# RG-LRU pieces handed to the engines in groups of four or five beside the RWKV recurrence, instead of one at a time

## The chip, the cores and the metric

The kernel runs on one core of one Trainium2 chip. The metric is the device time of one execution in microseconds (us), as the median of several. The names used for the engines are those of the profile: PE is the matmul engine (TensorE) and PEld its weight loads, DVE is VectorE, ACT is ScalarE, POOL is GpSimd, and SP is the engine that issues most transfers. Each engine runs its own instruction list strictly in order and waits for the others through semaphores.

## What is computed

One layer of a hybrid backbone over 128 context tokens and 1024 latent tokens, all in f32. A modulated input is projected; three mixers work on the columns of the projection (RWKV-7, RG-LRU and Mamba-2 SSD, each in both time directions); their outputs are projected, normalised, and sent through a mixture of 16 experts. Only two mixers matter here:

```python
# RWKV-7, per head and per direction, one step in time
sa = einsum('bhvk,bhk->bhv', s, -kk_t)
s = s * w_t + sa[..., None] * (kk_t * a_t) + v_t[..., None] * k_t
y_t = einsum('bhvk,bhk->bhv', s, r_t)
# RG-LRU, 768 channels, per direction
rg = sigmoid(blockdiag(w_a) @ xc + b_a);  ig = sigmoid(blockdiag(w_x) @ xc + b_x)     # xc: width-4 conv of xb
log_a = -8 * rg * softplus(-lam)
u = sqrt(-expm1(2 * log_a)) * (ig * xc)
h = linear_recurrence(exp(log_a), u, h0)          # h_t = a_t h_(t-1) + u_t
y = (h_forward + h_backward) * gelu(gb)
```

## The kernel before

The program runs nine stages one after the other, with a barrier between them: modulation, input projection, RWKV features, RWKV recurrence, RWKV output, SSD, output projection, experts, final norm. The change touches the recurrence stage alone (`rwkv_recurrence`), and in it only the second of its two runs: `rc` treats the 2 chunks of 64 context tokens with nothing beside it; `rs` treats the 16 chunks of latent tokens and computes the whole RG-LRU mixer (`Lru`) beside the recurrence.

**The recurrence.** Per chunk there are 25 named products, in this order: T Tt Bt A2 W2 X2 Y2 W4 X4 Y4 W8 X8 Y8 W16 vT X16 Y16 W32 R Y32 kT U bT Yo S. PE issues each for the two time directions one behind the other (chains g = 0 and 1). A plain product is 16 matmuls of 64x64 per direction; A2, R and S have twice as many and Yo three times. Every product has one taker that copies it out of PSUM: ACT for the X's and Y's, vT, kT, bT and Yo, DVE for all others. X needs the W of its level, the next W needs that X, and the next X and Y need the Y. `rs` gives three PSUM banks to each direction, so a product may not start before the one three places earlier has been taken. Every engine walks through the same 25 names of a chunk in the same order; one name of one chunk is a *slot*, 16 x 25 = 400 slots in all.

**The RG-LRU beside it.** `Lru` is written as one generator per engine, each of which yields 140 times: one opening piece, 23 pieces for each of six column blocks j, and one closing piece. Piece *j.v* of one engine belongs to piece *j.v* of the others, and semaphores join them. What a piece holds:

- v = 0 to 11: PE one gate product (128x128 weights, 384 columns, two PSUM banks in turn, so product w waits for the sigmoid of w-2) and ACT its sigmoid out of PSUM (L563). At v = 0 that sigmoid also waits for the output *y* of the block before. DVE does the four convolution steps of block j+1 at v = 3, 5, 7, 9; POOL multiplies at v = 6 and 12.
- v = 12 to 15, ACT on 128x1152: gelu and th0; th1 and av0; av1 and sq0; sq1.
- v = 15, 16, DVE: q0 (after sq0), q1 (after sq1). v = 16, 17, ACT: root0 (after q0), root1 (after q1).
- v = 17, DVE: u0 (after root0). v = 18: u1 (after root1) and the two scans of the forward direction. v = 19: the two scans of the backward direction. v = 20: two small copies and the sum. v = 21: y.
- SP loads the next inputs at v = 10, 12 and 22 and stores y at v = 22.

The opening piece computes constants (ACT, then DVE) and the whole convolution of block 0 (DVE).

`Aside` decides when pieces are issued. PE, ACT, DVE and POOL each own one and call its `turn()` once at the end of every slot, behind their instructions of that slot. So a piece's instructions stand in the engine's list between the recurrence's instructions of this slot and of the next. SP calls it 25 times in a row for each chunk, ahead of its wait for the end of that chunk and the loads of the chunk after next. Before the change `turn()` issues piece number floor(140 * slot / 400): one piece every two or three slots.

Of the kernel before, what the change touches and what calls it, by code (L numbers as in the profile page):

```python
# [73 lines left out]
class Chain:  # L74
# [5 lines left out]
    def turn(self, i, start=0):  # L80

        self.n, self.base = 0, start + i * self.per
# [334 lines left out]
class Aside:  # L417
# [5 lines left out]
    def turn(self):  # L423

        self.slot += 1
        while self.piece < self.pieces * self.slot // self.slots:
            self.piece += 1
            next(self.program)
# [249 lines left out]
def ssd(nc, d):  # L678
# [8 lines left out]
    with ExitStack() as stack:  # L687
# [156 lines left out]
        with ExitStack() as inner:  # L844
# [26 lines left out]
            def skewed(first, second, third, eng):  # L871

                def turn(c, b):
                    first(c + 1, 1 - b)
                    third(c - 1, 1 - b)
                    second(c, b)
                first(0, 0)
                first(1, 1)
                second(0, 0)
                with eng.Fori(0, NT // 2 - 1) as i:  # L880
                    for b in range(2):
                        turn(2 * i + b + 1, 1 - b)
                turn(NT - 2, 1)
                third(NT - 2, 1)
                second(NT - 1, 0)
                third(NT - 1, 0)
# [1266 lines left out]
def routing(nc, d, keep, raw, raw_in):  # L2153
# [3 lines left out]
    with ExitStack() as stack:  # L2157
# [56 lines left out]
        def _(pe):  # L2214
# [22 lines left out]
            def turn_gates(t):  # L2237
                pe.wait_ge(dve_g.sem, dve_g.at("aff", t))
                if t:
                    pe.wait_ge(dve_a.sem, dve_a.at("affT", t - 1))  # L2240
                pe_a.done(pe.transpose(ap[0:E, 0:P], aff[:, t % 2], ident[:]), "affT")
            turn(0)
            for t in range(NT):
                if t + 1 < NT:
# [624 lines left out]
```

## Time and profile before

| | before |
|---|---|
| median of three runs | 5324.62 us (5320.96 to 5327.24) |
| profiled execution, its time | 5324.72 us |
| its span in the trace | 5323.0 us |
| `rs`, first matmul to the last instruction on DVE's state | 1793 to 2406 us, 613 us |
| share of busy time in the whole span | PE 80%, PEld 63%, DVE 46%, ACT 29%, POOL 10% |

The span is what the trace covers; 1.7 us of the execution lie around it. The busy shares are means over nine stages with different limits. What is changed lies in the 613 us of `rs`, 11.5% of the span.

### The profile page before, as it was taken

What the parts mean: (1) busy time and instruction counts of PE and PEld (TensorE: products, weight loads), DVE (VectorE), ACT (ScalarE), POOL (GpSimd) and SP (SyncE); (2) the same over time, 40 slices, a digit from 0 to 9 for tenths busy, and PEclk for the clock granted to TensorE, in tenths of its full rate; (3) what the DMA queues carried; (4) which work ended last, traced back from release to release, by engine and by line L of the source; (5) the groups of instructions that cost most, each with busy time, mean ns of one, the idle gap of its engine ahead of it and who ended that gap; (6) DMA issues with size and microseconds to landing.
All of it is one profiled execution on the core that took longest, in us unless ns stands there. A gap on an engine that the chain in (4) does not pass through costs nothing. (4 is left out here: it accounts for less than half of the span.)

```text
span 5323.0 us, 87271 instructions
## 1 busy us (share of the span) xinstructions
PE 4268.0 (80%) x38736; PEld 3342.1 (63%) x38736; DVE 2439.8 (46%) x2312; ACT 1553.5 (29%) x1654; POOL 514.2 (10%) x298
## 2 busy tenths in 40 slices
PE   4599999998444789992265699974999999999990
PEld 1599999998112688881154344463777777777760
DVE  2410010010664355454665232327666666666667
ACT  0111111110221254450222100012555555555540
POOL 0200000000132111111010000000010100101003
PEclk7799999999666899996556899976999999999995
DMA  8522222221776222223521631144888888988876
GB/s 317 186 73 62 62 73 63 62 73 41 283 285 230 62 56 73 56 48 110 158 80 36 225 112 67 70 150 159 290 299 295 295 298 294 304 291 297 295 240 244
DMA packets 560198, 893.45 MB, mean 168 GB/s; under 512 B 147123, under 2 KB 323663, under 8 KB 533375
## 3 DMA queue, kind: packets, MB, share of 16 engines
q1 hardware_dynamic: 517708, 794.76, 43.9%
q10 hardware_dynamic: 32964, 56.31, 2.8%
q0 software_dynamic: 9216, 37.75, 2.8%
q8 instruction: 255, 4.18, 0.3%
q14 instruction: 55, 0.44, 0.0%
HBM read 745.15 MB, written 143.58 MB: 167 GB/s over the span
## 5 line engine op out<-in xcount | busy, mean ns | idle before, releaser
L2615 DVE TENSOR_TENSOR ex_lo<-moe_raw,ex_hi 128x2048 fp32r<-128x2048 f32 x384 | 879.7, 2291 | 417.0 <-ACT ex_hi L2551 416.8
L2551 ACT ACTIVATE ex_hi<-moe_raw 128x2048 fp32r<-128x2048 f32 x384 | 735.4, 1915 | 578.3 <-PE ex_bank L2493 351.6
L379 PE MATMUL feat_acc<-proj_hH,feat_wH 128*128 128x384 f32 x2112 | 706.5, 335 | 12.6 <-DVE feat_wL L362 12.6
L379 PE MATMUL feat_acc<-proj_hL,feat_wH 128*128 128x384 f32 x2112 | 706.3, 334 | 0.0
L379 PE MATMUL feat_acc<-proj_hH,feat_wL 128*128 128x384 f32 x2112 | 706.2, 334 | 0.0
L362 DVE TENSOR_TENSOR feat_wL<-proj_raw,feat_wH 128x2048 fp32r<-128x2048 f32 (+1 forms) x44 | 99.0, 2253 | 962.1 <-ACT feat_wH L334 962.1
L2090 PE MATMUL op_acc<-op_w,op_yT 128*128 128x512 f32 x1152 | 496.5, 594 | 25.3 <-DMA op_w<-in_w_out 25.3
L2090 PEld LDWEIGHTS op_acc<-op_w,op_yT 128*128 128x128 f32 x1152 | 219.5, 191 | 301.8 <-issue 301.8
L379 PEld LDWEIGHTS feat_acc<-proj_hH,feat_wH 128*128 128x128 f32 x2112 | 397.1, 188 | 13.0 <-DVE feat_wL L362 13.0
L379 PEld LDWEIGHTS feat_acc<-proj_hL,feat_wH 128*128 128x128 f32 x2112 | 397.1, 188 | 0.0
L379 PEld LDWEIGHTS feat_acc<-proj_hH,feat_wL 128*128 128x128 f32 x2112 | 397.0, 188 | 0.0
L2493 PE MATMUL ex_bank<-ex_hi,ex_xH 128*128 128x512 f32 x1024 | 328.2, 402 | 14.5 <-DVE ex_lo L2615 12.9
L340 ACT ACTIVATE feat_out<-feat_acc 128x1152 f32<-128x1152 f32 (+1 forms) x44 | 49.9, 1135 | 938.6 <-PE feat_acc L379 938.6
L2493 PE MATMUL ex_bank<-ex_lo,ex_xH 128*128 128x512 f32 x1024 | 317.2, 391 | 0.0
L2493 PE MATMUL ex_bank<-ex_hi,ex_xL 128*128 128x512 f32 x1024 | 316.2, 390 | 0.0
L2493 PEld LDWEIGHTS ex_bank<-ex_hi,ex_xH 128*128 128x128 f32 x1024 | 184.2, 188 | 83.9 <-issue 27.6
L2515 PE MATMUL ex_bank<-moe_raw,ex_xce 128*32 128x256 f32 x4096 | 234.3, 381 | 0.0
L2493 PEld LDWEIGHTS ex_bank<-ex_lo,ex_xH 128*128 128x128 f32 x1024 | 192.8, 188 | 41.8
L2493 PEld LDWEIGHTS ex_bank<-ex_hi,ex_xL 128*128 128x128 f32 x1024 | 192.6, 188 | 41.4
L2515 PEld LDWEIGHTS ex_bank<-moe_raw,ex_xce 128*32 128x32 f32 x4096 | 126.6, 110 | 99.5 <-issue 22.5
L1434 PE MATMUL rf_mod_acc<-rf_wq,rf_sil 128*32 128x512 f32 x512 | 88.8, 798 | 124.7 <-DMA rf_wq<-in_w_mod 124.7
L2493 PE MATMUL ex_bank<-ex_hi,ex_hH 128*128 128x512 f32 x512 | 167.5, 408 | 0.0
(417 smaller groups left out, 6083.7 us busy)
## 6 DMA issues: line engine op xcount, KB each, us to landing
moe_raw<-in_w_gate SPq DMA_DIRECT2D x256, 512.0 KB, 8.2
moe_raw<-in_w_up SPq DMA_DIRECT2D x256, 512.0 KB, 9.9
moe_raw<-in_w_down SPq DMA_DIRECT2D x256, 512.0 KB, 7.4
rf_wq<-in_w_mod SPq DMA_DIRECT2D x64, 1024.0 KB, 9.9
proj_raw<-in_w_in SPq DMA_DIRECT2D x43, 1024.0 KB, 5.5
mod_slab<-in_w_mod SPq DMA_DIRECT2D x8, 4096.0 KB, 30.9
scratch_FEAT<-feat_out ACTq DMA_DIRECT2D x43, 576.0 KB, 2.8
rr_feat<-scratch_RW SPq DMA_DIRECT2D x144, 128.0 KB, 3.0
```

What stands on the lines that cost most here:

```text
L340: act.activation(out[0:m, k].rearrange("p (g c) -> p g c", g=NSEG), acc[k][0:m, :, 0:SEG], ACT.Copy).then_inc(copied, 1)
L362: dve.tensor_tensor(wL[:, k, :, 0:m], raw[:, k, :, 0:m], wH[:, k, :, 0:m], ALU.subtract).then_inc(low, 1)
L379: last = pe.matmul(acc[k][:, g, 0:SEG], a[:, k, t, :], b[:, t, cols], start=t == 0 and j == 0, stop=t == KT - 1 and j == 2)
L1434: last = pe.matmul(mod_acc[j % 2][32 * g:32 * g + 32, :], sil[:, k, :], wq[:, u % MRING, g * MW:(g + 1) * MW], start=k == 0, stop=k == KT ...
L2090: last = pe.matmul(acc[slot][:, q, :], yT[:, slot, k, :], w[:, k, q * 512:(q + 1) * 512], start=k == 0, stop=k == KT - 1)
L2493: last = pe.matmul(main(ph)[b][:], m[:, k, :], w[:, slot, a, 512 * b:512 * (b + 1)], start=i == 0 and a == 0 and j == 0, stop=i == top and ...
L2515: last = pe.matmul(ctx(ph)[32 * j:32 * j + 32, 0:256], x, raw[:, n % NRAW, a, 256 * j:256 * (j + 1)], start=i == 0 and a == 0, stop=i == t ...
L2551: act.activation(hi[:, n % NS], raw[:, n % NRAW], ACT.Copy).then_inc(hi_made, 1)
L2615: dve.tensor_tensor(lo[:, n % NS], raw[:, n % NRAW], hi[:, n % NS], ALU.subtract).then_inc(lo_made, 1)
```

## The change

Two lines are added in `Aside.turn`. A slot whose number is not a multiple of twelve now issues nothing, except the last, number 400. At slots 12, 24, ..., 396 and 400 the loop catches up, so that each engine issues four or five pieces (the first group four with the opening piece; the last two) one behind the other.

```diff
@@ class Aside
     def turn(self):
         self.slot += 1
+        if self.slot % 12 and self.slot < self.slots:
+            return
         while self.piece < self.pieces * self.slot // self.slots:
             self.piece += 1
             next(self.program)
```

As 12 does not divide 25, the groups fall behind changing names of the chunk. Which pieces each group holds (slot, product of that slot, pieces; the groups that hold only pieces v = 0 to 11 are left out):

```
 12 X8   opening, 0.0-0.2      192 Y16  2.16-2.19            312 X8   4.12-4.15
 48 bT   0.11-0.14             204 A2   2.20-2.22, 3.0       324 Yo   4.16-4.19
 60 Y4   0.15-0.19             240 vT   3.9-3.13             336 W8   4.20-4.22, 5.0
 72 U    0.20-0.22, 1.0        252 Tt   3.14-3.17            372 U    5.10-5.13
108 W4   1.9-1.12              264 W16  3.18-3.21            384 X4   5.14-5.17
120 Y32  1.13-1.17             276 T    3.22, 4.0-4.2        396 kT   5.18-5.21
132 Y2   1.18-1.21             144 R    1.22, 2.0-2.2        400 S    5.22, closing
180 W2   2.11-2.15
```

No instruction is added or removed, and the order of each engine's pieces among themselves stays.

## Rows read from the trace of the kernel before

**Rows 1.** Busy time by stretch: us, PE, PEld, DVE, ACT, POOL, PE clock, DMA, GB/s.
```profile
1793.00:2406.00 613.00, 553.95 (x15505) 500.80 (x15505) 307.95 (x586) 289.44 (x570) 88.40 (x80) 0.95 0.25 61
...
1900.60:1904.60 4.00, 3.99 (x74) 3.99 (x76) 1.76 (x4) 1.41 (x4) 0.00 (x0) 0.50 0.01 4
```

**Rows 2.** Waits of PE, 1790 to 2410: total us, times, longest us.
```profile
PE rs_bank L1709 <- DVE rr_W L1837: 34.2, 17, 10.8
PE rs_bank L1709 <- DMA rr_rt<-scratch_RT: 9.5, 1, 9.5
PE rs_bank L1709 <- ACT rr_X L1779: 8.9, 4, 4.8
PE rs_bank L1709 <- ACT rr_Y L1779: 8.1, 4, 2.9
PE rs_bank L1709 <- issue: 2.7, 7, 0.5
PE rs_bank L1709 <- DVE rr_Tt L1830: 2.3, 3, 1.4
PE rs_bank L1709 <- DVE rr_U L1839: 1.0, 1, 1.0
```

**Rows 3.** Timeline of PE at the stage's start: start, us, idle before.
```profile
1811.26 1.97 PE L1709 MATMUL rs_bank<-rr_W,rr_Y 64*64 64x64 f32 x32 [10.75 <-DVE rr_W L1837]
```

**Rows 4.** Timeline of DVE around the scans of block 0.
```profile
1893.76 1.35 DVE L635 TENSOR_TENSOR lru_th<-lru_th,lru_ig 128x1152 f32<-128x1152 f32 x1
1895.02 0.42 DVE L643 TENSOR_TENSOR_SCAN lru_rg<-lru_av,lru_th 128x128 f32<-128x128 f32 x1
...
1897.60 0.40 DVE L643 TENSOR_TENSOR_SCAN lru_rg<-lru_av,lru_th 128x128 f32<-128x128 f32 x1
...
1900.16 0.73 DVE L1837 TENSOR_TENSOR rr_W<-rs_bank,rr_masks 128x256 f32<-128x256 f32 x2
```

**Rows 5.** Timeline of PE behind the same scans.
```profile
1900.61 1.97 PE L1709 MATMUL rs_bank<-rr_W,rr_Y 64*64 64x64 f32 x32 [4.17 <-DVE rr_W L1837]
...
1905.73 1.10 PE L1709 MATMUL rs_bank<-rr_ident,rr_feat 64*64 64x64 f32 x32
1906.67 1.10 PE L1709 MATMUL rs_bank<-rr_W,rr_Y 64*64 64x64 f32 x32
...
1908.53 1.10 PE L1709 MATMUL rs_bank<-rr_X,rr_Tt 64*64 64x64 f32 x32
```

**Rows 6.** Timeline of ACT over pieces 0.12 and 0.13.
```profile
1865.16 1.28 ACT L567 ACT_TABLE_LOAD   x1
...
1868.67 0.64 ACT L1779 ACTIVATE rr_X<-rs_bank 128x256 f32<-128x256 f32 x2
...
1869.72 1.27 ACT L572 ACTIVATE lru_th<-lru_rg,lru_sp 128x1152 f32<-128x1152 f32 x1
...
1873.47 0.64 ACT L1779 ACTIVATE rr_Y<-rs_bank 128x256 f32<-128x256 f32 x2
```

**Rows 7.** Instruction groups by shape in the stage: busy us, mean ns, idle before.
```profile
L563 ACT ACTIVATE lru_rg<-lru_bank,lru_bias 128x384 f32<-128x384 f32 x36 | 20.9, 581 | 46.9 <-PE lru_bank L534 46.8
...
L584 ACT ACTIVATE lru_th<-lru_th 128x1152 f32<-128x1152 f32 x12 | 13.9, 1164 | 5.2 <-DVE lru_th L651 5.1
...
L651 DVE SCALAR_TENSOR_TENSOR lru_th<-lru_rg,lru_th 128x1152 f32<-128x1152 f32 x12 | 16.7, 1394 | 1.6 <-ACT lru_rg L577 1.4 <-ACT lru_rg L580 0.2
...
L613 DVE SCALAR_TENSOR_TENSOR lru_cv<-lru_xb,lru_par,lru_cv 128x1155 f32<-128x1155 f32 x12 | 17.8, 1484 | 0.1
```

**Rows 8.** Timeline of PE around one gate product.
```profile
1817.86 1.15 PE L1709 MATMUL rs_bank<-rr_W,rr_Y 64*64 64x64 f32 x32
1818.93 0.91 PE L534 MATMUL lru_bank<-lru_xc,lru_gates 128*128 128x384 f32 x2
1819.78 1.15 PE L1709 MATMUL rs_bank<-rr_Y,rr_W 64*64 64x64 f32 x32
```

**Rows 9.** The page's costliest groups: matmuls of the same width back to back.
```profile
L379 PE MATMUL feat_acc<-proj_hH,feat_wH 128*128 128x384 f32 x2112 | 706.5, 335 | 12.6 <-DVE feat_wL L362 12.6
```

## The prediction

> **What bounds the kernel now.** Only the 613 us of `rs` can change, so I read the windows first: PE is busy for 554 of them, at a mean granted clock of 0.95 [rows 1]. So PE sets the time, and what the change can give or take is PE's idle time, the clock behind it, and the price of single PE instructions. Next come PE's waits: 66.7 us in seven lines [rows 2]. Of these 9.5 are the first load, which stays. The longest wait for DVE, 10.75 us, stands at the first W product, while the opening piece runs [rows 3]. The other 46.4 us are what today's spread pieces cost in idle time. The timeline shows how one of them arises. u1 and the four scans of block 0 occupy DVE from 1893.76 to 1900.16, 6.4 us in one lump; W8 stands behind them in DVE's list, is taken at 1900.16, and PE goes on at 1900.61 after 4.17 us of idling [rows 4, 5]. So a lump on DVE is hidden as far as PE has products that don't need it, here 2.2 us, and the rest is lost. PE is then slow too: the granted clock is 0.50, the 1.2 GHz level [rows 1], and three products take 5.12 us, where the next three take 2.80 [rows 5], so 2.3 us more are lost. A plain product thus costs 0.93 us for both directions, A2, R and S 1.87, Yo 2.8.
>
> A check of this reading: 21 plain products, three double and one triple make 28 us, with some 1 us of short waits 29 per chunk and 464 for 16. A gate product delays PE by 1.92 - 0.93 = 0.99 us [rows 8], 72 of them 71. Idle time behind the first load is 57. A clock of 0.95 means 61 us at the low level; some 17 of those are the opening, and at the rate of 2.3 lost of 5.1 the others cost 20. The sum is 612 of 613 us.
>
> **The change, part by part.** No instruction comes or goes; what changes is how many pieces stand in a row between two slots.
>
> *Groups with pieces 0 to 11 only.* PE has four or five gate products in a row, and ACT four or five sigmoids of 0.58 us [rows 7]. PE isn't idle there, so DVE's one or two convolution steps, at most 1.48 us each [rows 7], are hidden behind about 3.2 us of gate products. Without that cover each pair would cost up to 3 us. Gate products behind each other can save PE something. Nothing saved is one bound. The other is the projection's matmul of the same width, 335 ns in a stream [rows 9]; a gate product is two such instructions, 0.67 us, which saves 0.32. Between them stands the chain of two banks: a gate product of 0.91 [rows 8], its sigmoid of 0.58 and some 0.05 of signalling make 1.54 per two, so 0.77, which saves 0.2. I take that: 72 products in 23 groups leave 49 that follow another, 49 x 0.2 = -10 us (0 to -16).
>
> *The opening.* It moves from slot 3 to slot 12, by when its loads have landed. But ACT's constants now stand behind the taking of X8. From the end of X8: 0.6 for the taking, 2.0 on ACT (a table load of 1.28 [rows 6] and three short steps), 0.9 for five short steps on DVE and 5.3 for the convolution (four steps of at most 1.48 [rows 7], the first and last shorter), then a late first sigmoid, 1.1; the short ones are estimates. That is 10 us against 10.75 [rows 3]: 0 (-3 to +3).
>
> *Heavy groups.* Prices on ACT: v = 12 takes 3.5 us from its table load to the next taking, v = 13 3.75 [rows 6]; v = 14 2.3 and v = 15 1.15 at the same pace; a table load and root0 1.28 + 1.16 [rows 6, 7]. On DVE: q and u 1.35 each [rows 4, 7], two scans 2.58 [rows 4], v = 20 1.5 and v = 21 1.3, by the same width. I count from the end of the slot's product on PE; taking it ends some 0.6 later (an estimate from 0.73 us for both directions [rows 4], the first of which is taken while the second is multiplied). From the start of a taking to the matmul that needs it is 0.45 us [rows 4, 5].
>
> Three groups in full. **Slot 60 (Y4, pieces 0.15 to 0.19)**: ACT 0.6, sq1 1.15, load and root0 2.44, so 4.2; DVE then u0, to 5.5, and the lump of 6.4, to 11.9; only then does it take W8. PE has W8 to multiply, 0.93, and X8 needs it taken: idle 11.9 + 0.45 - 0.93 = 11. **Slot 120 (Y32, 1.13 to 1.17)**: ACT 0.6, th1, load, av0, av1, sq0, to 6.6; q0 on DVE to 7.9; load and root0 to 10.4; u0 to 11.7. Behind these stand the takings of kT and U. PE has kT, U and bT, 2.8, and Yo needs U: 9.5. **Slot 132 (Y2, 1.18 to 1.21)**: DVE has u1, four scans, the sum and y, 9.3 us, in front of W4. It began behind W2; PE has X2, Y2 and W4: 7.
>
> The others in the same way. ACT's lump in front of Yo (slot 48): 5; of X4 (108): 2.5; X2 (180): 10; X16 (240): 6; bT (372): 4.5. Both engines in turn, in front of W32 (192): 8.5; Bt (252): 5, as DVE has no slack there; W16 (312): 9; S (324): 9.5; W8 (384): 6.5. DVE alone in front of W32 (264): 4.5; of U (396): 6.5. The groups in which y meets the next block's first sigmoid (72, 204, 336): 1, 2, 3; a sigmoid table load in front of two waiting gate products (144, 276): 1 each. Together with 11, 9.5 and 7 that is 113 us against 46.4 today: **+67**. If PE covers 1 us more or less in each of the 20, 20 us either way.
>
> *Clock.* Fourteen of these stalls are over 4 us, like that of rows 5, and I charge each 2.3 us: 32, against the 20 of today: **+12** (0, if no stall adds a low stretch, to +20). The Trainium skill, "TensorE: Matmul & The Clock Gate", section "Why this matters for your kernels", advises against idle gaps between bursts of matmuls because the clock falls back; by it every heavy group, not fourteen, would be charged, some 14 us more. The trace agrees for the gap of 4.17 us and shows the clock restored within six.
>
> The table loads are as many as before. The same skill, "ScalarE: Activation LUTs", section "What ACT_TABLE_LOAD costs", puts 2.66 us on a switch, drain included; by it the loads in my lumps would cost some 20 us more. The row shows 1.28 us, with the next work right behind [rows 6], and the sum goes by it.
>
> *SP and POOL.* SP issues its pieces ahead, before the end of the chunk; grouping delays them by at most eleven slots, and the nearest use (gb from v = 22 to v = 12 of the next block) is more than thirty slots off. POOL's multiplications are used four pieces later or more. Both at 0, by that distance; a load that came late would stop PE for its few us once per block.
>
> **Sum.** 67 + 12 - 10 + 0 = +69. The profiled execution took 5324.7 us, span and 1.7 us around it, as the median of the three runs does: 5324.7 + 69 = **5394 us**.
>
> **The rivals.**
> *Half of it is covered.* What ACT does in the lumps might be hidden by PE's look-ahead of three banks, so that only DVE's lumps count. The five ACT groups (28 us) and about 15 of the mixed ones would go: 5394 - 43 = 5351. For it: ACT waits for PE most of the time. Against it: X's wait for ACT reached 4.8 us [rows 2] with single pieces already. Chance 0.08.
> *Faster: one interruption instead of four.* Place: PE at the 23 groups with gate products. Their spacing falls to 0.67, 16 us less, and a group would disturb the level chain once where four pieces do so four times. It decides as soon as the stalls sum to under 62 us, 3 per heavy group instead of 5.6; with today's 46 the time is 5324.7 - 16 = 5309. For it: 34.2 us of waits for DVE in 17 places [rows 2]. Against it: most of today's pieces cost nothing, as one alone fits into the 2.2 us that PE covers, and four don't. Chance 0.07.
> *The clock doesn't come back.* Stalls come every 12 to 25 slots; where two follow each other closely the clock may stay low throughout the products between. Twelve products cost 11 us at full clock, and at the rate of rows 5 some 9 more; for the ten groups that follow a stall, less the 2.3 charged, +67: 5461. Against it: three products were enough. Chance 0.04.
> *Nothing changes*, since the waits in the pieces order the engines whatever their place: 5325. PE's idling at the lumps speaks against it. Chance 0.03.
>
> **How the numbers follow.** My forecast has 0.78. Its own terms reach from 67 - 20 - 16 - 3 + 0 = +28 to 67 + 20 + 3 + 20 = +110, and not all ends meet. The range 5350 to 5440 takes in the half-covered case and leaves out the clock's, the faster one's, no change and the tails, together 2 in 10. A difference of 0.2% (10.6 us) is about what a measurement of this kernel can tell from none. Faster 0.06 (the faster rival, where it exceeds that bound), same 0.04, slower 0.90.
>
> **What the profile after would show.** PE's waits in `rs` at about 133 us in place of 66.7, in some 20 places of 2 to 11 us at the slots named, the longest behind slot 60; the mean clock of the stage near 0.93; gate products 0.8 us apart inside a group; the same busy times on ACT, DVE and POOL; the other stages unmoved. The prediction is wrong if the lumps run while PE is still busy (PE's waits near 66 us), if the gate products gain more than they lose, or if the opening stalls PE for much more than 10 us.

## The result, and the profile after

The changed kernel takes 5407.8 us against 5323.4, 1.0163 times as long (95% interval 1.0145 to 1.0181); measured again beside later experiments, 1.0155 (1.0136 to 1.0175). It is 84 us slower, where 69 were forecast, and inside the range.

`rs` as a whole, by the windows (columns as in [rows 1]):

```profile
1790.00:2485.60 695.60, 560.67 (x15505) 516.24 (x15505) 312.14 (x587) 292.50 (x570) 84.33 (x80) 0.90 0.22 54
```

The stage now takes 695.5 us instead of 613.1, so it holds the whole loss. The busy times of DVE and ACT are nearly what they were (312 and 293 us against 308 and 289); the mean granted clock went from 0.95 [rows 1] to 0.90. PE's waits, which answer to [rows 2]:

```profile
PE rs_bank L1711 <- DVE rr_W L1839: 63.1, 20, 11.3
PE rs_bank L1711 <- ACT rr_X L1781: 20.2, 4, 9.8
PE rs_bank L1711 <- DVE rr_U L1841: 15.4, 2, 9.0
PE rs_bank L1711 <- DMA rr_rt<-scratch_RT: 9.5, 1, 9.5
PE lru_bank L536 <- DVE lru_xc L623: 8.6, 1, 8.6
PE rs_bank L1711 <- DVE rr_S L1846: 8.2, 1, 8.2
PE rs_bank L1711 <- ACT rr_yo L1773: 4.8, 1, 4.8
PE rs_bank L1711 <- issue: 4.6, 5, 2.3
PE rs_bank L1711 <- ACT rr_bT L1781: 4.5, 1, 4.5
PE lru_bank L536 <- ACT lru_rg L565: 2.7, 2, 1.4
```

They sum to 141.6 us instead of 66.7, and they name new places: S, Yo and bT, takings that stand behind a group; U rises from 1.0 to 15.4. The timeline of PE at some of them (idle time before the instruction in brackets):

```profile
1845.58 1.15 PE L1711 MATMUL rs_bank<-rr_W,rr_Y 64*64 64x64 f32 x32 [1.51 <-DVE rr_W L1839]
...
1903.76 1.98 PE L1711 MATMUL rs_bank<-rr_W,rr_Y 64*64 64x64 f32 x32 [11.28 <-DVE rr_W L1839]
...
1936.77 1.15 PE L1711 MATMUL rs_bank<-rr_W,rr_Y 64*64 64x64 f32 x32
1937.85 3.14 PE L536 MATMUL lru_bank<-lru_xc,lru_gates 128*128 128x384 f32 x8
1940.92 1.15 PE L1711 MATMUL rs_bank<-rr_Y,rr_W 64*64 64x64 f32 x32
...
2003.64 0.48 PE L1711 MATMUL rs_bank<-rr_A,rr_U 64*64 64x64 f32 x4 [9.02 <-DVE rr_U L1841]
...
2026.54 1.97 PE L1711 MATMUL rs_bank<-rr_W,rr_Y 64*64 64x64 f32 x32 [6.94 <-DVE rr_W L1839]
...
2190.69 1.23 PE L1711 MATMUL rs_bank<-rr_W,rr_Y 64*64 64x64 f32 x32 [2.74 <-DVE rr_W L1839]
```

The three groups worked out in full, slots 60, 120 and 132, were forecast at 11, 9.5 and 7 us and measure 11.28, 9.02 and 6.94. Four gate products in a row take 1940.92 - 1937.85 = 3.07 us, 0.77 each. Counted as [rows 8] were, from the product ahead to the one behind, they delay PE by 1940.92 - 1936.77 - 0.93 = 3.22 us, where four single ones cost 4 x 0.99 = 3.96. What the stall behind slot 60 is made of shows on ACT and DVE, whose lines alternate:

```profile
1891.87 1.25 ACT L582 ACTIVATE lru_rg<-lru_rg,lru_nsp 128x1152 f32<-128x1152 f32 x1
1893.13 1.28 ACT L586 ACT_TABLE_LOAD   x1
1894.43 2.22 ACT L586 ACTIVATE lru_th<-lru_th 128x1152 f32<-128x1152 f32 x2
```
```profile
1893.15 1.36 DVE L653 SCALAR_TENSOR_TENSOR lru_th<-lru_rg,lru_th 128x1152 f32<-128x1152 f32 x1 [2.01 <-ACT lru_rg L582]
1895.62 2.63 DVE L637 TENSOR_TENSOR lru_th<-lru_th,lru_ig 128x1152 f32<-128x1152 f32 x2 [1.12 <-ACT lru_th L586]
1898.17 0.42 DVE L645 TENSOR_TENSOR_SCAN lru_rg<-lru_av,lru_th 128x128 f32<-128x128 f32 x1
...
1903.30 0.73 DVE L1839 TENSOR_TENSOR rr_W<-rs_bank,rr_masks 128x256 f32<-128x256 f32 x2
```

sq1, the load and the roots on ACT; q1, u0, u1 and the scans on DVE, each waiting for the other; then W8 is taken, at 1903.30.

To compare kernels I split the stage of each profiled execution in three, by windows of 2 us: PE idle; PE busy at the low clock level, counted as busy time x (1 - granted clock); and the rest, which is PE's work at full clock. Time outside the stage differs by up to 30 us between executions, whatever the kernel, so the stage says more than the total where little is at stake.

| us | stage | idle | lost to the clock | rest |
|---|---|---|---|---|
| before | 613.1 | 59.1 | 22.1 | 531.9 |
| after | 695.5 | 134.8 | 42.1 | 518.6 |
| after, again | 690.1 | 135.0 | 34.8 | 520.3 |
| only gate products grouped | 615.9 | 72.2 | 21.2 | 522.5 |
| only long pieces grouped | 678.0 | 119.1 | 31.9 | 527.0 |
| groups every six slots | 638.2 | 84.6 | 30.5 | 523.1 |
| after, PE kept busy | 672.0 | 61.4 | 12.7 | 597.8 |
| after, short scans | 664.3 | 109.1 | 35.0 | 520.3 |
| after, 2.11 earlier | 683.3 | 127.3 | 35.8 | 520.2 |
| gates only, short POOL work | 617.1 | 70.6 | 24.0 | 522.6 |
| placed | 553.2 | 25.0 | 3.0 | 525.1 |
| placed, tables earlier | 549.1 | 18.3 | 2.9 | 527.9 |

Between before and after: idle +75.7, clock +20.0, rest -13.3, together +82.4. The loss of the clock varies with the execution, as the repeat shows; idle time and rest don't.

### The profile page after: what moved, and what is told of

It is laid out like the page before. It is cut to its first block and busy times, and to the rows that moved or that the text cites. A ratio compares the mean times of both kernels' runs of the same rounds, so it can differ in the third digit from the quotient of the medians.

```text
span 5406.2 us, 87271 instructions
## 1 busy us (share of the span) xinstructions
PE 4289.3 (79%) x38736; PEld 3368.9 (62%) x38736; DVE 2444.3 (45%) x2312; ACT 1556.4 (29%) x1654; POOL 510.4 (9%) x298
## 5 line engine op out<-in xcount | busy, mean ns | idle before, releaser
L1436 PE MATMUL rf_mod_acc<-rf_wq,rf_sil 128*32 128x512 f32 x512 | 92.2, 828 | 119.1 <-DMA rf_wq<-in_w_mod 119.1
```

The source lines that it names most:

```text
L1436: last = pe.matmul(mod_acc[j % 2][32 * g:32 * g + 32, :], sil[:, k, :], wq[:, u % MRING, g * MW:(g + 1) * MW], start=k == 0, stop=k == KT ...
```

## The experiments

Where pieces are given other slots, a table replaces the formula (`UPTO`, the number of pieces issued by the end of each slot; `self.slots` is 400 here):

```diff
-        while self.piece < self.pieces * self.slot // self.slots:
+        while self.slots == 400 and self.piece < self.pieces and UPTO[self.slot] > self.piece:
```

**Only the gate products, only the long pieces.** In the first, pieces v = 0 to 11 go to multiples of twelve (at the latest with v = 12), in the second v = 12 to 22. In both the opening piece stays at slot 3.

> Only the pieces v = 0 to 11 are collected at multiples of twelve slots; v = 12 to 22 stay one at a time. Theory (what costs is the lump of long ACT and DVE work in front of an awaited taking; gate products in a row are 0.79 us apart instead of 0.99): 48 of 72 gate products follow another, -10 us, idle time of PE near the 66.7 us of before, so 5314 us (5305 to 5322). Rival (every interruption costs, whatever it holds, so fewer turns are better): about 17 us less idle time as well, 5297. Rival (groups of gate products stall PE at their two banks): slower than before, 5335 or more.

> Only the pieces v = 12 to 22 are collected at multiples of twelve slots; gate products are issued one at a time. Theory (the long lumps carry the whole loss, the gate groups gave 10 us back): the time after plus 10, 5418 us (5405 to 5430), with PE's waits near 140 us. Rival (the gate groups carry the loss): 5325 to 5340.

Gates alone: 1.0008 (0.9997 to 1.0019). Long pieces alone: 1.0127 (1.0108 to 1.0145), some 68 of the 84 us (in the stage 64.9 of 82.4), and the gate groups don't carry the loss. Neither met its number. With gates alone the rest fell by 9.4 us, close to the 10 expected, but idle time rose by 13.1. Its waits:

```profile
PE rs_bank L1729 <- DVE rr_W L1857: 40.3, 20, 9.3
PE rs_bank L1729 <- ACT rr_Y L1799: 10.6, 4, 2.7
...
PE lru_bank L554 <- ACT lru_rg L583: 3.6, 3, 1.4
```

W's wait for DVE is up by 6.1 against [rows 2], Y's for ACT by 2.5, and 3.6 are new: a gate product that waits for a sigmoid behind its table load. So groups of short pieces aren't free either; what they save they lose again. With long pieces alone I expected more than after, and the stage is 17.5 us shorter: 15.7 of idle time and 10.2 of clock less, 8.4 of the rest more. One place explains half of the idle time: W4 behind slot 180 waits 1.66 us there, 9.79 after. ACT before these two waits, first after, then with the long pieces alone:

```profile
2088.16 0.37 ACTq L1777 DMA_DIRECT2D scratch_YD<-rr_yo  x1
2096.42 0.58 ACT L565 ACTIVATE lru_ig<-lru_bank,lru_bias 128x384 f32<-128x384 f32 x1 [8.29 <-PE lru_bank L536]
2097.02 1.28 ACT L569 ACT_TABLE_LOAD   x1
...
2107.67 0.63 ACT L1781 ACTIVATE rr_X<-rs_bank 128x256 f32<-128x256 f32 x2
```
```profile
2089.65 0.37 ACTq L1795 DMA_DIRECT2D scratch_YD<-rr_yo  x1
2090.04 1.28 ACT L587 ACT_TABLE_LOAD   x1 [0.43 <-ACT rr_yo L1791]
```

After, ACT idles 8.29 us in front of a sigmoid, whose gate product stands behind W2 in PE's list, and 10 us of long work wait behind that sigmoid. Without the sigmoid ACT begins at once. That was tested by moving this one piece.

**One piece moved.** 2.11 joins the group of slot 168. The changed kernel ran beside it on the same chip.

> The kernel after with one piece moved: 2.11, a gate product and its sigmoid, goes with the group of slot 168 instead of slot 180. Theory (at slot 180 ACT had been free since Yo, but the sigmoid of 2.11 must wait for a gate product that stands behind W2 in PE's list, and the 12 us of long work stand behind that sigmoid; without it they start some 8 us earlier): the stall of 9.8 us at W4 shrinks to about 1.7, as it did where only the long pieces were grouped, and a low-clock stretch goes, 10 us less than the kernel after. Rival (the lump is as long as before, whoever stands in front): no difference beyond 2 us.

> The kernel after, beside the others on the same chip, so that the move of one piece can be told from it: 1.0145 to 1.0181 of the kernel before, by the first measurement.

5397.1 against 5405.7, 8.6 us less, idle time 7.7 less. The totals' intervals (1.0115 to 1.0159 and 1.0136 to 1.0175) overlap, so the place tells more: the taking of X2 is no longer late, as ACT's load starts at 2087.51 and W4 waits 1.62 us. The low clock behind W4 is gone too (1.00 from 2098.7 to 2110, against 0.50 behind W4 in the repeat of after), but the stage as a whole lost no less to the clock (35.8 against 34.8), so in the sum that gain isn't seen.

```profile
2087.51 1.28 ACT L587 ACT_TABLE_LOAD   x1 [0.43 <-ACT rr_yo L1791]
```
```profile
2098.67 1.15 PE L1729 MATMUL rs_bank<-rr_X,rr_Tt 64*64 64x64 f32 x32 [1.62 <-ACT rr_X L1799]
```

**Groups half as large.** `self.slot % 6` in place of 12.

> Groups every six slots, two or three pieces each. Theory (PE covers some 2 to 5 us of a lump, and only what exceeds that is lost): half-size lumps lose little more than single pieces; idle +10, clock +5, gate products -7, so 5331 us (5315 to 5360). Rival (the loss is proportional to the group's size): 5323 + 84 x (2.1 - 1) / (4.2 - 1) = 5352.

5345.0, a ratio of 1.0039 (1.0021 to 1.0057), or 21 us (11 to 30). The theory's 8 lies below this interval, the proportional 29 just inside it, and the expected range took in both. The stage has 25.5 us more idle time than before, where proportion to the group's size gives 75.7 x 1.1 / 3.2 = 26.0, and 8.4 more lost to the clock; the rest is 8.8 shorter. So half-size groups are not free, and that a lump costs little up to some size isn't shown: here the sum of idle time goes with the size of the groups.

**Shorter lumps.**

```diff
-                for lo, w, name in ((0, TC, f"hc{r}"), (TC, TS, f"hs{r}")):
+                for lo, w, name in ((0, 8, f"hc{r}"), (TC, 8, f"hs{r}")):
```

> The kernel after with the four scans of each block cut to 8 of their 128 and 1024 columns, so the states and the output of RG-LRU are not computed. Theory (a microsecond of lump in front of an awaited taking costs a microsecond): the lumps behind slots 60, 132, 192, 264, 324 and 396 shrink by 4.8 us each, which takes about 29 us of idle time and some 4 us of slow clock: 5375 us (5365 to 5385). Rival (a group costs a fixed price for its interruption): 5408 within 5.

5382.8, a ratio of 1.0103 (1.0082 to 1.0124): 57 us above its runs of before where after stood 84 above its own, so about 27 less; idle time 25.7 less. In place, from the first scan to the taking behind the last it is 0.44 us instead of 5.13, so 4.69 less, and the stalls behind slots 60, 132, 192, 324 and 396 are each shorter by 4.68 or 4.69; the 4.55 behind 264 are gone. A fixed price per group is refuted; a microsecond of lump costs a microsecond as long as there is a stall left.

**PE kept busy.** In front of each of the 14 long stalls (arguments are left out at `...`):

```diff
                             if side:
                                 side.turn()
+                                if side.slot in WARM:
+                                    pe.wait_ge(other.gated, ...)
+                                for _ in range(WARM.get(side.slot, 0)):
+                                    pe.matmul(other.bank[0][:, 384:512], ..., start=True, stop=True)
```

> The kernel after, with matmuls that nobody reads (128x128 weights, 128 columns) placed where PE stalled for more than 4 us in the trace after, in number for all but 0.8 us of each of the 14 stalls. Theory (the stall also costs the slow clock behind it; 42 us are lost at the low level in the stage after, 22 before): most of the 14 low stretches go, 25 us less, 5383 us (5372 to 5395). Rival (only the idle time costs, the clock nothing beside it): 5408, or some us more where the added matmuls overrun a stall.

5385.9, a ratio of 1.0113 (1.0096 to 1.0130), so 22 to 27 us less than after with 644 more matmul instructions. The rest of 597.8 us in the table holds the added matmuls. The loss to the clock fell from 42.1 to 12.7. The slow clock behind the stalls thus costs about 25 us by itself. Behind slot 60 the clock fell all the same, to 0.50 from 1898.7 to 1901.7, after the added 8.75 us and an idle gap of 2.60:

```profile
1887.36 8.75 PE L1756 MATMUL lru_bank<-rr_masks 128*128 128x128 f32 x76
...
1898.70 1.98 PE L1714 MATMUL rs_bank<-rr_W,rr_Y 64*64 64x64 f32 x32 [2.60 <-DVE rr_W L1847]
```

**POOL's part in the small waits.** The gates-only kernel with 64 columns in `pool.tensor_tensor`.

> The kernel with only the gate pieces grouped, and the two POOL multiplications of each block cut to 64 of 1152 columns, so that RG-LRU's input gate is applied to those columns alone. Theory (POOL's multiplication, which the groups place behind Yo, slows DVE's update of S from 0.42 to 1.37 us, and a wait of 1.5 us follows at W2): the update takes 0.42 us throughout, the wait of 1.5 us goes, 1 to 5 us less in all. Rival (the slow update has another cause, for example where the chunk begins): it stays at 1.37.

The update of S takes at most 428 ns, and W's wait for DVE falls from 40.3 to 35.8, so POOL's work is the cause of the slow update. The wait of 1.5 us in front of X2 of chunk 1 (chunks counted from 0) shrinks to 0.81 and doesn't go; the larger gain is in front of X2 of chunk 9, where a slow convolution step is gone too and 2.77 us become 0.47. But waits for which the trace names no releaser rise from 1.5 to 5.2 us, and the time is 1.0009 (0.9995 to 1.0023), no different; what POOL's work costs isn't resolved.

**Placed by room.**

> A slot written out for each piece: gate products in groups of four behind W16, Y16 and Y32; v = 12 and 13 behind Yo, where ACT has no taking for some 8 us; the forward scans behind U, where DVE has none for 5 us; the rest singly behind takings with 2 to 3 us of room; the opening behind U of chunk 0. Theory (only place and size of a lump count): idle time of PE from 66.7 to about 27 us, clock loss from 22 to about 8, gate products -11: 5323 - 40 - 14 - 11 = 5258 us (5245 to 5285). Rival (grouping as such costs, by its interruption of the chain): above 5323.

5264.5, a ratio of 0.9882 (0.9866 to 0.9898): 1.2% faster than the kernel before, 63 us where 65 were expected. The sum is closer than its parts: PE's waits are 36.6 us less where 40 were expected, the clock's loss 19.1 where 14 were, the rest 6.8 where 11 were. Its windows and waits:

```profile
1785.50:2339.00 553.50, 528.12 (x15505) 484.70 (x15505) 309.23 (x588) 290.16 (x570) 84.10 (x80) 0.99 0.28 67
```
```profile
PE rs_bank L1728 <- DVE rr_W L1856: 9.4, 18, 1.5
PE rs_bank L1728 <- DMA rr_rt<-scratch_RT: 9.3, 1, 9.3
PE lru_bank L553 <- ACT lru_rg L582: 6.8, 5, 1.4
```

The longest wait behind the first load is 1.5 us, and the clock is 0.99. It has groups too, 7.3 us of ACT work in one lump among them (1930.89 to 1938.22); they stand where the engine has no taking to do, and here ACT still waits for PE behind the lump:

```profile
1930.89 1.28 ACT L586 ACT_TABLE_LOAD   x1 [0.43 <-ACT rr_yo L1790]
...
1936.96 1.26 ACT L592 ACTIVATE lru_av<-lru_rg,lru_nsp 128x1152 f32<-128x1152 f32 x1
1939.04 0.85 ACT L1798 ACTIVATE rr_X<-rs_bank 128x256 f32<-128x256 f32 x2 [0.83 <-PE rs_bank L1728]
```

The 6.8 us that gate products wait for a sigmoid led to one more:

> The placed schedule with the first gate product of each block two slots earlier, alone behind X8, and the others moved up by one. Theory (five waits of 1.4 us, 6.8 in all, are a gate product waiting for a sigmoid behind a table load): about 5 us less than the placed schedule, 5254 to 5262. Rival (the load then delays the taking of Y8 by as much): no difference.

The waits are gone and the stage is 4.1 us shorter, near the 5 expected. The total, 5269.2, missed its 5254 to 5262; its ratio (0.9895, 0.9873 to 0.9917) can't be told from the other's.

## Why the prediction was right

**The heavy groups** were the main term, and it holds place by place. Of the 20 stalls that I listed, 113 us, the trace shows 110: at 13 of them within 0.3 us, the largest misses at slots 324 (8.2 instead of 9.5) and 336 (1.6 instead of 3). At slot 72 I count nothing, where 1 was forecast; a wait of 2.3 us ahead of Bt, six products on, has no releaser in the trace and may belong to it. The counting rule, the lump's end less the products that PE can still issue, was sound, and short scans and the moved piece support it from both sides. The opening stalled 8.6 us, 10 forecast.

**The gate groups** were mis-sized in both directions. The term for PE's spacing, -10, measured between -9.4 and -13.3; the rest also fell by 4.9 with the long pieces alone, where most gate products stay single, so it tells the spacing to some 5 us. But the step "PE isn't idle there" failed: some 13 us of waits stand outside my list. Of these 9.0 are in front of X2 in twelve chunks, the longest 1.5 in chunk 1 and 2.7 in chunk 9, where convolution steps, POOL's multiplication and the takings of the chunk's first products meet on DVE; for 4.6, the 2.3 ahead of Bt among them, no cause is shown. With gates alone idle time rises by 13.1 over before, at the same two places (1.5 and 2.8) and at others. So this part comes to about nothing, not to a gain of 10.

**The clock** was charged 12 us more than before and took 20 (13 in the repeat); kept busy, PE gets back about 25 us. Added up by stretches of low clock, the fourteen long stalls cost 32.1 us, 2.3 each, as charged (28.4 in the repeat). What the charge left out are short waits: behind waits of 2.3, 2.6 and 2.7 us (ahead of Bt, in front of W8 and X2) the clock was 0.50 as well, which makes 5.1 us more:

```profile
1928.80:1932.20 3.40, 3.40 (x66) 3.40 (x68) 1.12 (x2) 0.00 (x0) 0.00 (x0) 0.50 0.73 162
1980.00:1983.40 3.40, 3.40 (x71) 3.40 (x68) 0.85 (x2) 0.89 (x4) 0.00 (x0) 0.50 0.03 5
2191.70:2195.00 3.30, 3.30 (x68) 3.30 (x66) 0.42 (x1) 1.25 (x4) 0.00 (x0) 0.50 0.00 0
```

The trace before had such stretches already: eight of its ten behind the opening follow waits of 1.9 to 3.0 us, and the ten cost 18.1, not 20. The Trainium skill ("TensorE: Matmul & The Clock Gate", section "Why this matters for your kernels") advises against idle gaps above a length that it names. The trace agrees for the long stalls (0.50 from 1903.8 to 1908.3, behind slot 60). My shortest stalls lie below that length, so the 26 us that I drew from the Trainium skill, with every heavy group charged, do not follow from it. The mean granted clock of the stage is 0.90, idle time included; I forecast 0.93.

**SP and POOL** at nothing: no wait of PE for a load is new. POOL's is not quite nothing, as the slow update of S and the slow convolution step in chunk 9 show.

**The rivals.** That half is covered by PE's look-ahead is refuted at the ACT groups: 4.8, 2.6, 9.8, 6.3 and 4.5 us of stall, where it needed none. That one interruption is cheaper than four is refuted by the gates alone, no faster, and by the six-slot groups. The clock came back behind each stall after at most 5.9 us of PE's work; the rival in which it doesn't would have taken 50 us more. The forecast's total was 14 us low by the median (5407.8 against 5394). By the profile it is 13 of unlisted waits and 8 of clock, less 3 in the stalls, 2 at the opening and 3 at the rest, which makes 13 us; the table closes on the stage's 82 us.

## What to carry to other kernels

Filler work in an in-order engine is free only as far as the engine that sets the pace has work that needs none of what stands behind the filler; read that room from the idle time in front of each taking, and put lumps by size into rooms by size. Grouping is neither good nor bad: the same pieces made the kernel 1.6% slower behind every twelfth product and 1.2% faster where they had room. Look at what stands first in a group: one short instruction that waits for another engine holds up all long work behind it, even where that would have fitted.

## What the runs showed of the hardware

A POOL multiplication of 128x1152 stretched some of the DVE operations that met it. The update of S before, after, with gates alone, and the same with POOL's work cut (columns: shortest, median, longest ns); one update of the 36 was slow, the one that began at 1837.94 while POOL multiplied from 1836.40 to 1839.03:

```profile
L1844 DVE TENSOR_TENSOR rr_S<-rr_Stmp,rr_pc x36: 424/424/427, 1740.6 to 2406.0; 128x256 f32<-128x256 f32 x36
```
```profile
L1846 DVE TENSOR_TENSOR rr_S<-rr_Stmp,rr_pc x36: 424/426/1372, 1736.4 to 2485.3; 128x256 f32<-128x256 f32 x36
```
```profile
L1864 DVE TENSOR_TENSOR rr_S<-rr_Stmp,rr_pc x36: 424/425/1368, 1737.9 to 2406.9; 128x256 f32<-128x256 f32 x36
```
```profile
L1864 DVE TENSOR_TENSOR rr_S<-rr_Stmp,rr_pc x36: 424/425/428, 1738.1 to 2408.0; 128x256 f32<-128x256 f32 x36
```

A convolution step met one in chunk 9 and took 3.8 us; after, and with POOL's work cut:

```profile
L615 DVE SCALAR_TENSOR_TENSOR lru_cv<-lru_xb,lru_par,lru_cv x12: 1414/1423/3809, 1810.0 to 2306.8; 128x1155 f32<-128x1155 f32 x12
```
```profile
L633 DVE SCALAR_TENSOR_TENSOR lru_cv<-lru_xb,lru_par,lru_cv x12: 1415/1423/1506, 1803.2 to 2257.0; 128x1155 f32<-128x1155 f32 x12
```

Not every operation is stretched: those that read `rs_bank`, in PSUM, and ran during such a multiplication kept their usual time within 2% in the traces before, after and with gates alone. The two slow ones read only SBUF; that this decides is not tested.

The second surprise is the clock's loss: two executions of the same kernel with the same idle time, 134.8 and 135.0 us, lost 42.1 and 34.8 us to it, so two profiles that differ by some 7 us there need not differ in the kernel.
